# Layer one's query and key projections: both parts of x in one moving row of 512 columns

## The reference

```
h   = rms_norm(x, g0)
qkv = h @ w_qkv                       # 1024 x 3072, 16 heads
z   = q @ k.T * 64**-0.5
log_stay = where(s < t, log_sigmoid(-z), 0)
log_a = log_sigmoid(z) + reverse cumulative sum of log_stay over the later keys
o   = where(s < t, exp(log_a), 0) @ v
x   = x + rms_norm(o @ w_o, g1)
x   = x + rms_norm(swiglu(rms_norm(x, g2)), g3)
```

## Time and profile before

| | |
|---|---|
| median of the runs | 772.78 us (772.66 to 773.12) |
| the profiled execution | 771.64 us |
| its span, first to last instruction | 770.0 us |
| TensorE busy | 761.4 us, 4495 matmuls |
| VectorE busy | 503.9 us, 674 instructions |
| ScalarE busy | 397.5 us, 536 instructions |
| GpSimd busy | 113.2 us, 173 instructions |
| mean granted clock of TensorE | 0.997 of full speed |

### The profile page before, as it was taken

One profiled execution on the slowest core, in us unless ns is written; L12 is line 12 of the kernel. 1 busy time (PEld: TensorE's weight loads), 2 busy tenths in 40 slices (PEclk: granted clock), 3 DMA queues, 4 the chain that ended last, 5 costly groups with the idle time before them and its releaser, 6 DMA issues.

```text
span 770.0 us, 12712 instructions
## 1 busy us (share of the span) xinstructions
PE 761.4 (99%) x4495; PEld 655.3 (85%) x4495; DVE 503.9 (65%) x674; ACT 397.5 (52%) x536; POOL 113.2 (15%) x173
## 2 busy tenths in 40 slices
PE   9999999999999999999999999999999999999996
PEld 7999977888888888999889898898888888888885
DVE  5788987675455455878667668668647755554543
ACT  4766667453343343855665666556645434333421
POOL 3000001610000000314325235233002000000000
PEclk9999999999999999999999999999999999999998
DMA  8635585785654554659686685684643856556502
GB/s 250 185 106 160 190 247 191 232 263 196 214 190 163 176 192 123 169 150 230 171 221 152 163 232 136 161 237 163 217 137 112 298 170 205 172 195 210 194 1 55
DMA packets 157441, 139.16 MB, mean 181 GB/s; under 512 B 6616, under 2 KB 147008, under 8 KB 157408
## 3 DMA queue, kind: packets, MB, share of 16 engines
q1 hardware_dynamic: 153440, 131.55, 55.1%
q0 software_dynamic: 3712, 6.88, 4.8%
q10 hardware_dynamic: 256, 0.30, 0.1%
HBM read 137.60 MB, written 1.11 MB: 180 GB/s over the span
## 4 chain that ended last, share of the span: by engine, by line
PE 95%; DVE 1%; ACT 1%; DMA 1%; issue 0%; DVEq 0%; POOLq 0%; SPq 0%; POOL 0%; ACTq 0%
PE ps L1165 21%; PE ps L1167 20%; PE ps L1166 20%; PE ps L1416 10%; PE ps L1418 5%; PE ps L1171 2%; PE ps L1173 2%; PE ps L1172 2%; PE ps L1474 1%; PE ps L1330 1%; DMA raw<-in_w_qkv_a 1%; PE ps L1444 1%; PE ps L1483 1%; PE ps L1218 1%; PE ps L1260 1%; PE ps L1186 1%
## 5 line engine op out<-in xcount | busy, mean ns | idle before, releaser
L780 DVE TENSOR_TENSOR w_lo<-raw,w_hi 128x2048 fp32r<-128x2048 f32 (+2 forms) x144 | 279.4, 1956 | 45.9 <-ACT w_hi L500 44.2
L500 ACT ACTIVATE w_hi<-raw 128x2048 fp32r<-128x2048 f32 (+2 forms) x144 | 232.6, 1636 | 51.0 <-DMA raw<-in_w_kv_b 20.7
L1165 PE MATMUL ps<-w_hi,xt 128*128 128x512 f32 x352 | 139.6, 397 | 0.0
L1167 PE MATMUL ps<-w_hi,xt 128*128 128x512 f32 x352 | 137.5, 391 | 0.0
L1166 PE MATMUL ps<-w_lo,xt 128*128 128x512 f32 x352 | 137.2, 390 | 0.0
L665 ACT ACTIVATE work<-ps,stat 128x256 f32<-128x256 f32 x44 | 20.9, 476 | 199.4 <-PE ps L1167 199.4
L1165 PE MATMUL ps<-w_hi,ot 128*128 128x512 f32 x240 | 95.0, 396 | 0.4 <-DVE w_lo L780 0.4
L1167 PE MATMUL ps<-w_hi,ot 128*128 128x512 f32 x240 | 93.6, 390 | 0.0
L1166 PE MATMUL ps<-w_lo,ot 128*128 128x512 f32 x240 | 93.6, 390 | 0.0
L1167 PEld LDWEIGHTS ps<-w_hi,xt 128*128 128x128 f32 x352 | 66.1, 188 | 13.9
L1165 PEld LDWEIGHTS ps<-w_hi,xt 128*128 128x128 f32 x352 | 66.2, 188 | 13.5 <-issue 0.6
(11 more groups left out here) (148 smaller groups left out, 1245.3 us busy)
## 6 DMA issues: line engine op xcount, KB each, us to landing
raw<-in_w_gate_up SPq DMA_DIRECT2D x88, 512.0 KB, 4.8
raw<-in_w_kv_b SPq DMA_DIRECT2D x96, 256.0 KB, 3.9
raw<-in_w_down SPq DMA_DIRECT2D x22, 1024.0 KB, 4.9
raw<-in_w_q_b SPq DMA_DIRECT2D x48, 256.0 KB, 4.1
raw<-in_w_qkv_a SPq DMA_DIRECT2D x23, 512.0 KB, 4.9
raw<-in_w_o_a SPq DMA_DIRECT2D x4, 1024.0 KB, 6.8
work<-bias_rows POOLq DMA_DIRECT2D x64, 64.0 KB, 3.6
raw<-in_w_o_b SPq DMA_DIRECT2D x4, 1024.0 KB, 5.3
```

The lines of the kernel that those rows point to most:

```text
L500: act.activation(w_hi[:, s % CUT, 0:size(s)], raw[:, s % RAW, 0:size(s)], ACT.Copy).then_inc(hi_made, 1)
L780: dve.tensor_tensor(w_lo[:, c, 0:n], raw[:, s % RAW, 0:n], w_hi[:, c, 0:n].bitcast(F32), ALU.subtract).then_inc(lo_made, 1)
L1165: mm(out, xs[0], ws[0], start=start, stop=False)
L1167: return mm(out, xs[1], ws[0], start=False, stop=stop)
```

## The change

For pairs 1 to 7, queries and keys are each projected into a bank of their own, queries into bank 0 and keys into bank 1. For each of the eight slices of the sum, one matmul with the high weights moves both parts of x, 512 columns, so that the first half of the bank gets high x high and the second high x low; then eight matmuls of 256 columns with the low weights are added to the first half. ScalarE copies the second half of each bank to `low` (two `low_a` per pair, before and behind `between[0]`), and VectorE adds it to the first half and then multiplies the sum where it lies. `low` is one tile, so the copy for the keys waits until VectorE has read that for the queries. Pair 0 is taken as before, under the name `take_first_a`.

```diff
+            def low_a(p, j, c):
+
+                act.wait_ge(w_used, j * 6 + query_a(p) + c + 1)
+                if c or not isinstance(j, int) or p >= 2:
+                    act.wait_ge(lowa_used, j * 4 + 2 * (p - 1) + c)
+                act.activation(low, bank(c, SEQ, SEQ), ACT.Copy).then_inc(lowa_made, 1)
...
                 act.activation(spl_cut[0], spl, ACT.Copy).then_inc(spl_hi, 1)
+                if not isinstance(j, int) or a < PAIRS - 1:
+                    low_a(a + 1, j, 0)
                 between[0]()
+                if not isinstance(j, int) or a < PAIRS - 1:
+                    low_a(a + 1, j, 1)
                 act.wait_ge(stay_made, j * 2 + a + 1)
...
-            def take_qk_a(p, j):
-                dve.wait_ge(*((w_used, j * 6 + query_a(p) + 2) if p else (first_used, 2)))
+            def take_first_a():
+                dve.wait_ge(first_used, 2)
                 dve.scalar_tensor_tensor(qa, bank(0, 0, SEQ), SCALE, rows[:, :], ALU.mult, ALU.mult)
                 dve.tensor_tensor(ka, bank(0, SEQ, SEQ), rows[:, :], ALU.mult).then_inc(qka_made, 1)
+
+            def take_qk_a(p, j):
+                for c, to in enumerate((qa, ka)):
+                    count = j * 4 + 2 * (p - 1) + c + 1
+                    dve.wait_ge(lowa_made, count)
+                    dve.tensor_tensor(to, bank(c, 0, SEQ), low, ALU.add).then_inc(lowa_used, 1)
+                    dve.wait_ge(lowa_used, count)
+                    if c == 0:
+                        dve.scalar_tensor_tensor(to, to, SCALE, rows[:, :], ALU.mult, ALU.mult)
+                    else:
+                        dve.tensor_tensor(to, to, rows[:, :], ALU.mult).then_inc(qka_made, 1)
...
-            def project_a(p, j, c, b, col, ks=range(KT)):
+            def project_a(p, j, c):
 
                 s = query_a(p) + c
                 pe.wait_ge(lo_made, j * 6 + s + 1)
                 w = cut_unit(s, k=KT)
-                for k in ks:
-                    inst = by_w(bank(b, col, SEQ), [v[:, k, :] for v in w], [xt[:, n, k, :] for n in range(2)],
-                                k == 0, k == KT - 1)
-                if k == KT - 1:
-                    inst.then_inc(w_used, 1)
+                both = bank(c).rearrange("p (n s) -> p n s", n=2)
+                for k in range(KT):
+                    mm(both, w[0][:, k, :], xt[:, :, k, :], start=k == 0, stop=False, skip_group_check=True)
+                for k in range(KT):
+                    inst = mm(bank(c, 0, SEQ), w[1][:, k, :], xt[:, 0, k, :], start=False, stop=k == KT - 1,
+                              skip_group_check=True)
+                inst.then_inc(w_used, 1)
```

More of the change, by code:

```diff
@@ L243, in build @@
         exact_made = sem("exact_made")
+        lowa_made, lowa_used = sem("lowa_made"), sem("lowa_used")
         job_done, qkb_made, vb_made, q1_done = (sem(n) for n in ("job_done", "qkb_made", "vb_made", "q1_done"))
@@ L1080, in _ @@
             take_rows(1)
-            take_qk_a(0, 0)
+            take_first_a()
             lo(A0 + 3)
@@ L1282, in step_a @@
                     outputs_a(p - 2, j)
-                project_a(p, j, 0, 0, 0)
-                project_a(p, j, 1, 0, SEQ)
+                project_a(p, j, 0)
+                project_a(p, j, 1)
                 sums_a(p - 1, j)
@@ L1546, in _ @@
             pe.wait_ge(exact_made, 1)
-            project_a(1, 0, 0, 0, 0)
-            project_a(1, 0, 1, 0, SEQ)
+            project_a(1, 0, 0)
+            project_a(1, 0, 1)
             sums_a(0, 0)
@@ L1557, in _ @@
             outputs_a(last - 2, 0)
-            project_a(last, 0, 0, 0, 0)
-            project_a(last, 0, 1, 0, SEQ)
+            project_a(last, 0, 0)
+            project_a(last, 0, 1)
             sums_a(last - 1, 0)
```

## The result

The changed kernel takes 780.18 us (median of six runs, 778.72 to 780.83) against 772.72 us before (six runs, 772.35 to 773.12): a ratio of 1.0094, 95% interval 1.0084 to 1.0105. It is slower, by 7.5 us. The forecast was 778.1 with a range of 775.6 to 781.2, so the time lies within the range, 2.1 us above the forecast. It is the time of a rival, the clock that falls in the new gap, which had been put at 780.1 us.

A forecast was written before the change was run, and what follows sets the result against it. TensorE was taken to set the time, with VectorE nearly as full in the changed stage. 2.35 us of creep plus 2.95 us of stall gave +5.3 us, 776.9, plus 1.1 us to the median: 778.1 us, range 775.6 to 781.2.

The forecast's parts named there:

- the clock that falls in the new gap: Rival, chance 0.26: 3.0 us without matmuls before the last scores lowers TensorE's clock, costing 0 to 4.1 us, middle 2.0; 780.1 us.
- VectorE is nearly full, TensorE's saving is lost: Stage from 29 to 105 us: VectorE idles 1.2 of 11.4 us a step; TensorE's 1.2 us saving is lost waiting for it.
- steps of 11.8: Expected sign in the changed kernel's trace: steps of 11.8 us, against 11.41 us read from the kernel before.
- The second copy waits for two cuts, VectorE for the copy: Ordinary steps: ScalarE's second copy stands behind both w_hi cuts, so VectorE subtracts the sums 0.75 us later.
- The creep, 2.35 us: Full steps before the last pair: spl starts later step by step, 0.57, 0.97, 1.37, 1.60, finally 2.35 us.
- The last term, 0.75 ahead of a 2048-wide cut: Last step, spl at 94.74 us: no idle ahead of it, so its shift grows from 1.60 to 2.35 us.
- The last pair, 2.95 us, scores at 104.8: Pair 7's scores wait for the second copy behind two 2048-wide cuts, starting at 104.8 instead of 99.47; stall 2.95 us.
- Nothing is given back, and nothing else is late: Behind this stage both engines keep their order and TensorE has no idle to absorb the delay: everything runs 5.3 us later.
- the slack of 0.9 us: Weight loads: a unit's load ends about 0.9 us before its w_hi cut is due, and that slack hardly shrinks.
- the rival of the late loads: Rival, chance 0.07: load slack gone, ScalarE holds the second copy up to 0.9 us a step for four steps; 781.7 us.
- A clock below 1.00 behind the gap: Sign that the forecast is wrong: TensorE's granted clock below 1.00 after the wait before the last scores.

## Why the prediction was right, and where not

*VectorE is nearly full, TensorE's saving is lost.* Right, and shown from both sides: with the adds alone the loss is whole (780.30) and the ordinary steps are as long, without them the wide matmuls gain about half a microsecond of the 1.2 (0.5 us in the medians, within noise, and 0.56 us in the trace up to the last scores). VectorE's room was a little larger than the forecast took: the steps are 11.68 us, where "steps of 11.8" were expected.

*The second copy waits for two cuts, VectorE for the copy.* Right. From the start of the spl cut on ScalarE to VectorE's subtraction of the sums it was 3.41 us before (61.70 to 65.11) and is 4.12 now (63.25 to 67.37): 0.71 us, worked out as 0.75. Moving the copy by one cut takes the creep away.

*The creep, 2.35 us.* Right in size, but the closeness is luck, by errors that cancel. spl of the last step moved from 94.74 to 97.40, 2.66 us. From the first full step's spl (38.20, was 37.34) the growth is 1.80 us, less than forecast. Part of that is the 0.71 instead of 0.75, and part that more could be given back ahead of spl than the 0.35 us of idle that the row shows: the row before it can overlap by 0.08 us. From L864 to spl it was 0.78 us (70.61 to 71.39) and is 0.35 (72.87 to 73.22), 0.43 us a step. The last term, 0.75 ahead of a 2048-wide cut, measured 0.74. The other 0.86 us were there before the first full step. 0.56 us of them stand already at pair 0's spl (24.80, was 24.24), ahead of the first copy: this execution started later. The other 0.30 us arise in pair 1's own step, where the copies and additions move L892's counterpart by 0.26 us and a load comes 0.2 us late. The profiles of the two runs with filled gaps, whose steps are the same, have only 0.1 us there. The forecast counted neither. Without the late start the creep is 2.1 us by this trace; the run with the old last pair puts it at 2.5 us in medians.

*The last pair, 2.95 us, scores at 104.8.* Right: they start at 105.06, wait 2.87 us, and from spl to scores it is 7.66 us where it was 4.73, 2.93 more. The stall is 2.7 us in medians.

*Nothing is given back, and nothing else is late.* The first held: behind this stage everything runs 8.0 us later (119.63 before, 127.63 now for the first row of L516, L517 now). The forecast said 5.3; the difference is the clock and the 0.3 us more of creep. Loads held ScalarE only once behind 26 us, for 0.2 us ahead of the first full step, as the slack of 0.9 us said. But two late loads of 0.4 us in the run with the additions alone cost about 0.5 us a step, so the rival of the late loads can take part in single executions.

*The clock.* This is the step that failed in the forecast of 778.1: it carried no term for TensorE's clock and left the fall as a rival at 0.26. A clock below 1.00 behind the gap was one of its own signs of being wrong, and it is there. One observation, the end of the trace, had it fall 2.6 us behind the last matmul, and the gap was forecast at 3.0; that row should have been weighed as the likelier case. The fall even came earlier than that row suggested, 1.2 us behind the last matmul of the sums. The price was put at 2.0 us between 0 and 4.1, and it is 2.2 to 2.5 by the filled gap and 2.4 by the traces (scores to outputs of pair 6, 5.16 us before and 7.58 after). The warning in the Trainium skill (TensorE: Matmul & The Clock Gate, section "Why this matters for your kernels") against idle gaps between bursts of matmuls is borne out by the gap of 2.87 us. The price was underestimated by no more than 0.5 us, and the sum 2.35 + 2.95 + 2.0 gives the 780.1 that was written for this case. That it lies 0.1 from the median is partly luck again: the range held the result only because it had been drawn up over this rival.

## What to carry to other kernels

When one engine's work is moved to an engine that is "65% busy", read the busy share of the stage, and read what stands ahead of the new instruction in its queue: here one copy of 0.4 us, placed behind two cuts, cost the creep, and the additions themselves nothing that could be measured. When a forecast leaves the matmul engine idle for some 3 us, include the fall of its clock in the sum (here it came once even with waits of 0.47 and 1.06 us); a few useless matmuls in the gap prevented it. And price the most that a change can give first: half or more of TensorE's 1.2 us had a second engine right behind it.

## What the runs showed of the hardware

A gap of 2.87 us cost 2.4 to 2.5 us more than itself, since the clock stayed at 1.2 GHz for 5.2 us of matmuls behind it (105.1 to 110.3). A 512-column matmul then starts every 0.43 us instead of 0.23. The price of the same gap differs between executions: with 2.86 us of it in the run with the additions alone, the clock was at 1.2 GHz only from 106.4 to 109.8 us and cost 1.6 us. With waits of 0.47 and 1.06 us, 1.2 us apart, the clock fell in the profiled run, when matmuls were already running again, and three of eleven runs show the lower mean clock; with 0.84 and 1.58 us, and a filled stretch between, it did not in the profiled one. So the length of one gap does not decide it alone, and the same kernel can go either way. This may also be what widens the spread: the changed kernel's runs cover 2.1 us, those of the kernel before beside them 0.8, and its two fastest (778.72 and 779.23) have the highest mean clock, 0.996 against 0.994 and 0.995. What exactly decides was not tried.
